# An output projection by seven quarter products, and the experts' rows turned back by TensorE

## The reference

```python
x = first_block(x, ...)
for i in range(2):                        # even layer, odd layer
    h_l = modulate(x, norm_mix[i], shift, scale)     # and the same for ctx
    m_l, m_c = even_mixer(...) @ w_out    # odd: only m_l is needed
    x = x + mod_l[2] * m_l                # the gated projection
    tok = modulate(x, norm_ffn[i], mod_l[3], mod_l[4])   # rms norm * (1 + scale) + shift
    f = hier_moe(tok, ...)                # router, then 16 experts, the best 2 of one group of 4
    x = x + mod_l[5] * f
```

## Time and profile before

| | |
|---|---|
| median of three runs | 2024.25 us (2022.09 to 2025.62) |
| profiled execution | 2020.34 us, its span 2018.6 us |
| mean granted clock of TensorE | 0.983 |
| even layer's projection, TensorE's matmuls | 1192.80 to 1279.80 us |
| odd layer's projection, its last matmul | ends at 1800.35 us |

### The profile page before, as it was taken

How to read it: one execution, slowest core, us unless ns; L and a number is a source line. 1 busy time by engine, 2 the same in 40 slices (tenths; PEclk the granted TensorE clock), 3 DMA queues, 4 the chain that set the end, 5 groups by cost and what they waited for, 6 DMA issues and landing times.

```text
span 2018.6 us, 28998 instructions
## 1 busy us (share of the span) xinstructions
PE 1891.2 (94%) x10950; PEld 1038.5 (51%) x10950; DVE 1187.0 (59%) x1908; ACT 642.7 (32%) x1274; POOL 262.8 (13%) x319
## 2 busy tenths in 40 slices
PE   7999999999999999999998999899997999989993
PEld 4554875544444444555645764633334678645330
DVE  2001777487787653358845644677757667456774
ACT  2011762200000001242313631256643556323551
POOL 3000110011111000012200012611102000051101
PEclk9999999999999999999999999999998989999997
DMA  8632100677666442311111011689965020148995
GB/s 260 169 84 84 54 12 22 219 253 258 235 236 239 147 174 97 133 42 42 42 42 63 1 36 73 266 335 362 363 239 202 1 84 2 35 157 354 387 416 199
DMA packets 108473, 323.89 MB, mean 160 GB/s; under 512 B 9063, under 2 KB 43015, under 8 KB 89904
## 3 DMA queue, kind: packets, MB, share of 16 engines
q1 hardware_dynamic: 77920, 190.56, 26.3%
q0 software_dynamic: 25024, 112.01, 15.6%
q10 hardware_dynamic: 5392, 19.47, 2.4%
HBM read 291.48 MB, written 35.76 MB: 162 GB/s over the span
## 4 chain that ended last, share of the span: by engine, by line
PE 71%; issue 7%; DMA 7%; DVE 6%; PEld 4%; PEldq 2%; ACT 1%; POOL 1%; POOLq 0%; DVEq 0%; SPq 0%; ACTq 0%
PE ps L3441 15%; PE ps L2060 6%; PE ps L466 6%; PE ps L2872 6%; PE ps L1190 5%; PE ps L1236 4%; PE ps L3242 4%; PE ps L1211 4%; DMA X<-moe_rows,row_token 4%; PE ps L364 3%; PE ps L335 2%; PE ps L2893 2%; PE ps L2036 2%; PEld ps L1783 2%; PE ps L1783 1%
## 5 line engine op out<-in xcount | busy, mean ns | idle before, releaser
L3441 PE MATMUL ps<-wide 128*128 128x512 f32 (+1 forms) x736 | 306.5, 575 | 1.9 <-issue 1.7
L3441 PEld LDWEIGHTS ps<-wide 128*128 128x128 f32 x736 | 138.3, 190 | 166.2 <-issue 164.1
L2872 PE MATMUL ps<-wide,X 128*32 x448 | 197.5, 594 | 2.1 <-DVE X L3043 2.1
L2872 PE MATMUL ps<-Z,X 128*32 128x512 f32 x1344 | 197.9, 594 | 0.0
L2060 PE MATMUL ps<-wide 128*128 128x512 f32 (+1 forms) x384 | 148.3, 543 | 0.5 <-issue 0.5
L1544 DVE SCALAR_TENSOR_TENSOR Z<-Z,wide 128x2048 f32<-128x2048 f32 x56 | 131.6, 2349 | 2.8
L1190 PE MATMUL ps<-T 64*128 64x256 f32 (+1 forms) x888 | 109.8, 377 | 8.7 <-DVE nm L1329 6.8
L1783 PE MATMUL ps<-wide 128*128 128x512 f32 x256 | 112.1, 595 | 2.1 <-issue 1.0
L744 ACT ACTIVATE T<-ps 128x512 f32<-128x512 f32 (+2 forms) x139 | 70.7, 536 | 128.2 <-PE ps L1783 109.8
L1261 ACT ACTIVATE T<-T,nm 128x768 f32<-128x768 f32 (+3 forms) x112 | 86.7, 775 | 77.5 <-DVE nm L1329 77.5
L2872 PEld LDWEIGHTS ps<-wide,X 128*32 128x32 f32 x448 | 47.0, 110 | 124.1 <-issue 124.1
(11 more groups left out here) (421 smaller groups left out, 3366.0 us busy)
## 6 DMA issues: line engine op xcount, KB each, us to landing
wide<-in_experts SPq DMA_DIRECT2D x64, 1024.0 KB, 9.7
Z<-in_mod_w POOLq DMA_DIRECT2D x32, 1024.0 KB, 5.2
T<-in_experts SPq DMA_DIRECT2D x32, 1024.0 KB, 11.8
X<-in_mod_w POOLq DMA_DIRECT2D x16, 1024.0 KB, 5.3
moe_out<-X ACTq DMA_DIRECT2D x28, 512.0 KB, 8.5
wide<-in_w_down SPq DMA_DIRECT2D x12, 1024.0 KB, 6.8
wide<-in_w_gate SPq DMA_DIRECT2D x22, 512.0 KB, 6.0
wide<-in_w_up SPq DMA_DIRECT2D x22, 512.0 KB, 6.9
```

The lines of the kernel that those rows point to most:

```text
L2872: last = pe.matmul(ps[rows, t % 2, :], mo.xT[:, c, rows], w_rows, start=(c == 0), stop=(c == DK - 1))
L3441: last = pe.matmul(self.gu.bank(u)[:, columns], w, self.rhs(c)[:, columns], start=(c == 0), stop=(c == DK - 1))
```

## The change

Three things are changed. **One**: in the even layer alone the gated projection becomes `GatedBySeven`. The product of the rows by `w_out` is split into quarters: even and odd row tiles by the two halves of the inner dimension, and `w_out` into four quarters of 512 x 512. Seven products of quarters, three of them of sums of quarters, are enough for the four quarters of the result. VectorE makes eight sums (S1 to S4 of the rows, 128x1536 each; T1 to T4 of the weights, 128x2048 each). ScalarE copies each P1 to the four places of the result that contain it; VectorE adds P2, P3, P6 and P5 from PSUM to these, multiplies each row by the gate and adds it to `X`, and then adds P7 and P4, each multiplied by the gate by itself. The adds form a chain: each waits for the one before. TensorE's order is P1 (before the meeting), P2, P3, P6, P5, then P7 and P4 pair by pair, with the turn of pair 0 after pair 1's, and that of pair 1 after pair 2's.

**Two**: in both layers GpSimd prepares no rows. TensorE turns the modulated `HT` back (`turn` of `RowStores`, units of four transposes, two units for a row tile): four units in `first_logits` in place of nine `keep_awake` matmuls, the others in the router in place of 16, and ahead of the drain that frees the slots. ScalarE copies each unit into the rows' place: four copies ahead of its takes of the last pair, two between the Exps, the rest after them. GpSimd stores the rows in the router's part, after `await_spilled`. The broadcast loads and VectorE's gains go. The wait for the gate rows moves from the stage's start to just ahead of the gating.

**Three**: the `late` transfer goes to ScalarE's queue, behind the last row's store.

The core of the diff:

```diff
 class GatedBySeven(Stage):                                 # new
+        self.PARTS = [(p, i) for p in ("P1", "P2", "P3", "P6", "P5") for i in range(n)] + [(p, i) for i in range(n) for p in ("P7", "P4")]
+    def tensor(self, pe):
...
+        self.after_sum(pe, "T4")
+        for i in range(n):
+            self.part(pe, "P7", i, self.s3, self.b12, 0 if i else 1)
+            self.part(pe, "P4", i, self.rows(1, 1), self.b21, 0 if i else 2)
+            if i:
+                self.norm.turn(pe, i - 1)
+        pe.drain().then_inc(k.weights_used, 2)
+        self.between(pe, self.norm)
+        self.norm.tensor(pe)
+    def vector(self, dve, ch):
...
+        for i in range(n):
+            gate = self.gates[:, 0 if 2 * i < ST else 1, :]
+            for row in (0, 1):
+                t = 2 * i + row
+                add(("gated", i, row), self.result(t), gate, ALU.mult)
+                add(("total", i, row), k.X[:, t, :], self.result(t))
+        for i in range(n):
+            gate, x = self.gates[:, 0 if 2 * i < ST else 1, :], k.X[:, 2 * i + 1, :]
+            self.after_part(dve, "P7", i)
+            multiply(("P7", i, "gated"), halves(self.product), twice("P7", i), halves(gate))
+            add(("P7", i, "total"), x, self.product)
+            if i:
+                self.norm.tile(dve, ch, 2 * i - 1)
+            self.after_part(dve, "P4", i)
+            multiply(("P4", i, "gated"), self.product[:, 0:512], self.bank("P4", i), gate[:, 0:512])
+            add(("P4", i, "total"), x[:, 0:512], self.product[:, 0:512])
+            self.norm.tile(dve, ch, 2 * i)
+            if i:
+                self.norm.take(dve, "dve", i - 1)
+        self.norm.tile(dve, ch, 2 * n - 1)
+        self.norm.vector(dve, ch)
 class RowAndTileNorm:
             if i == ST - 1:
                 act.dma_start(self.away[:, i, :], k.X[:, i, :]).then_inc(k.last_row_stored.sem, 16)
+                for dst, src in self.late:
+                    act.dma_start(dst, src).then_inc(k.last_row_stored.sem, 16)
...
-            if i == ST - 1:
-                for dst, src in self.late:
-                    pool.dma_start(dst, src).then_inc(k.small_landed.sem, 16)
 class RowStores(Stage):
+    def turn(self, pe, a, b):
+        k = self.k
+        for u in range(a, b):
+            t = self.norm.tiles[u // 2]
+            if u >= 2:
+                pe.wait_ge(k.rows_copied.sem, self.copied + u - 1)
+            for j in range(4):
+                last = pe.transpose(self.bank(u)[:, j * P:(j + 1) * P], k.HT[:, 4 * (u % 2) + j, t * P:(t + 1) * P], k.ident[:, :])
+            last.then_inc(k.rows_turned.sem, 1)
+    def copy(self, act, a, b):
...
+    def store(self, pool):
+        k = self.k
+        for i, t in enumerate(self.norm.tiles):
+            pool.wait_ge(k.rows_copied.sem, self.copied + 2 * i + 2)
+            pool.dma_start(self.rows_out[t * P:(t + 1) * P, :], self.place(i)).then_inc(k.rows_stored.sem, 16)
 class Router(Stage):
         for dst, src in self.rows_gate:
             pool.dma_start(dst, src).then_inc(k.small_landed.sem, 16)
+        self.stores.store(pool)
         self.stores.await_rows(pool)
...
         self.logits(pe, 0)
-        keep_awake(pe, k=self.k, bank=norm.banks.first + 3, n=9)
+        self.stores.last_banks_read(pe)
+        self.stores.turn(pe, 0, self.stores.FIRST)
...
         self.banks.filled(last)
+        self.stores.turn(pe, self.stores.FIRST, 2 * len(self.tiles))
         pe.drain().then_inc(k.places_free.sem, 1)
-        keep_awake(pe, k, 7, 16)
-        even.then = Linear(k, hT, DK, A["ev_w_out_2"][0], D, allt, gated_take(k.gatebc), ["dve"] * 12,
-                           norm=mod_sets(0, 1, True))
+        gate_rows = Loading(k, gate_loads(0, 2, 2))
+        even.then = GatedBySeven(k, A["ev_w_out_2"][0], allt, mod_sets(0, 1, True), k.gatebc, gate_rows.landed)
```

More of the change, by code:

```diff
@@ L321, in begin, with last_banks_read @@
                 pe.matmul(self.banks.bank(i)[:, 0:cn], self.lhs(k0 + c, t), w[:, c, :], start=(c == 0), stop=False)
+    def last_banks_read(self, pe):
+        self.banks.taken(pe, len(self.blocks) * len(self.tiles) - 2)
     def tensor(self, pe):
@@ L846, in scalar @@
                 self.take(act, "act", p)
+        if self.rows_copies:
+            self.rows_copies(act)
         for p in self.rest:
@@ L2394, in gpsimd, with landed, __init__ @@
             pool.dma_start(dst, src).then_inc(self.k.gate_rows.sem, 16)
[L2396 to L2397 removed]
+    def landed(self, eng):
+        eng.wait_ge(self.k.gate_rows.sem, self.base + 16 * len(self.pairs))
 class RowStores(Stage):
[L2405 removed]
+    FIRST = 4
+    def __init__(self, k, l, norm, rows_out, away):
         super().__init__(k)
         n = len(norm.tiles)
[L2408 to L2416 removed]
+        self.l, self.norm, self.rows_out, self.away = l, norm, rows_out, away
         self.consts = k.small_landed.reserve(64)
         self.stored, self.spilled = k.rows_stored.reserve(16 * n), k.spilled.reserve(16 * n)
+        self.turned, self.copied = k.rows_turned.reserve(2 * n), k.rows_copied.reserve(2 * n)
         self.n = n
@@ L2422, in place, with bank @@
         return self.k.Z[:, 5120 + D * i:5120 + D * (i + 1)]
+    def bank(self, u):
+        first = (1 if self.n == NT else 5) if u < self.FIRST else 5
+        return self.k.ps[:, first + u % 2, :]
+    def turn(self, pe, a, b):
[7 more added lines that the diff above has]
+            last.then_inc(k.rows_turned.sem, 1)
@@ L2424, in gpsimd, with await_copied @@
+    def copy(self, act, a, b):
+        k = self.k
+        for u in range(a, b):
+            act.wait_ge(k.rows_turned.sem, self.turned + u + 1)
+            act.activation(self.place(u // 2)[:, 512 * (u % 2):512 * (u % 2) + 512], self.bank(u), ACT.Copy).then_inc(k.rows_copied.sem, 1)
+    def await_copied(self, eng, u):
+        eng.wait_ge(self.k.rows_copied.sem, self.copied + u)
     def gpsimd(self, pool, ch):
         k, mo = self.k, self.k.mo
-        for dst, src in self.loads:
-            pool.dma_start(dst, src).then_inc(k.row_mods_landed.sem, 16)
@@ L2428, in gpsimd @@
         for dst, src in ((mo.iota, k.C["iota"]), (mo.token, k.C["token"]), (mo.before, k.C["before"]), (mo.pace, k.C["pace"][:, self.l, :])):
             pool.dma_start(dst, src).then_inc(k.small_landed.sem, 16)
-        pool.wait_ge(k.row_gains_ready.sem, self.ready + len(self.sets))
         for i, t in enumerate(self.norm.tiles):
-            gain, shift = self.sets[0 if t < ST else 1]
-            row = self.place(i)
             pool.wait_ge(k.norm_rows.sem, self.norm.rows + i + 1)
             pool.dma_start(self.away[:, t, :], k.X[:, t, :]).then_inc(k.spilled.sem, 16)
-            for c in range(0, D, 256):
-                ch.step(pool.tensor_tensor(row[:, c:c + 256], self.norm.hn[:, t, c:c + 256], gain[:, c:c + 256], ALU.mult))
-            ch.wait()
-            for c in range(0, D, 256):
-                ch.step(pool.tensor_tensor(row[:, c:c + 256], row[:, c:c + 256], shift[:, c:c + 256], ALU.add))
-            ch.wait()
-            pool.dma_start(self.rows_out[t * P:(t + 1) * P, :], row).then_inc(k.rows_stored.sem, 16)
@@ L2444, in vector @@
-    def vector(self, dve, ch):
+    def store(self, pool):
         k = self.k
-        dve.wait_ge(k.row_mods_landed.sem, self.landed + 16 * len(self.loads))
-        for gain, _ in self.sets:
-            dve.scalar_tensor_tensor(gain, gain, 1.0, self.gain, ALU.add, ALU.mult).then_inc(k.row_gains_ready.sem, 1)
+        for i, t in enumerate(self.norm.tiles):
+            pool.wait_ge(k.rows_copied.sem, self.copied + 2 * i + 2)
+            pool.dma_start(self.rows_out[t * P:(t + 1) * P, :], self.place(i)).then_inc(k.rows_stored.sem, 16)
@@ L2506, in tensor @@
         self.stores.norm.pair_taken(pe, len(self.tiles) // 2 - 1)
+        self.stores.await_copied(pe, self.stores.FIRST)
         self.logits(pe, 1)
@@ L2524, in scalar @@
             act.activation(to[:, 0:n, :], x[:, 0:n, :], ACT.Exp).then_inc(k.step_done.sem, 1)
+            if i == 0:
+                self.stores.copy(act, self.stores.FIRST, self.stores.FIRST + 2)
+        self.stores.copy(act, self.stores.FIRST + 2, 2 * n)
     def vector(self, dve, ch):
@@ L3840, in two_blocks, with row_stores @@
         k.expertgate = k.ring[:, 1:3, 1024:SLOT]
-        def row_stores(l, projection, sets):
-            mods = [[bc(scratch["mods"], D, (l * 2 + r) * 6144 + m * D) for m in (3, 4)] for r in range(sets)]
-            projection.row_stores = RowStores(k, l, projection.norm, bc(A["norm_ffn_2"], D, D * l), mods, scratch["h"][l], away)
-            return projection.row_stores
+        def row_stores(l, projection):
+            stores = RowStores(k, l, projection.norm, scratch["h"][l], away)
+            stores.last_banks_read = projection.last_banks_read
+            projection.norm.rows_copies = lambda act: stores.copy(act, 0, stores.FIRST)
+            projection.row_stores = stores
+            return stores
```

(2 more changed lines are left out.)

162 lines of the change are left out of this document (145 added, 17 removed).

## The result

The changed kernel takes 2030.64 us (median of 7 runs, 2028.27 to 2036.97); the kernel before, timed with it, 2022.09 us (7 runs). The ratio is 1.0037, 95% interval 1.0022 to 1.0051: slower by 4.4 to 10.3 us. The profiled execution has a span of 2033.9 us against 2018.6.

A forecast was written before the change was run, and what follows sets the result against it. It took TensorE to set the pace until 1280, then a relay between engines. Terms +3.1 +2.75 +0.4 +0.3 -1.0 -2.65 = +2.9 us, on the median of 2024.25, gave 2027; range 2018 to 2033.

The forecast's parts named there:

- The projection: Even layer to second logits: VectorE's twelve gating operations keep TensorE idle 11.7 us, eating the 10.3 saved; +3.1 us.
- The clock: Even layer after the idle stretch: half clock slows pair 2's products; +2.75 us, ends +1.6 and +5.1.
- the short wait: TensorE's 3.1 us wait ending at 842.6, kernel before: full clock back 3.3 us on, losing 1.65 at half speed.
- the long wait: TensorE's 9.2 us wait, kernel before: full clock back 6.9 us after resuming at 1528.5, losing 3.45 at half speed.
- rival (b): Even layer: clock stays low through pair 2, logits, part of dispatch; +9 to +12 us, 2030 to 2033; chance 0.17.
- Router: Even router and dispatch: small operations gain 1.2 us, turns and cold keep-awakes cost; between -1.1 and +1.7, taken +0.4.
- the odd layer: Odd layer: last turn and logits stay near their times, router gains 1.2 us, cold keep-awakes give back some; -1.0.
- The barrier: Ahead of the even layer: moved transfer frees the barrier, -1.85 us; with a clock that may not fall, -2.65.
- The stores: Router, both layers: six stores near 1297 to 1301, gather about 1314, leaving 10 us; nothing to +2, taken +0.3.
- rival (c): Router: rows land after the token list and the gather waits, +2 to +4 us, 2030; chance 0.05.

The follow-up runs named there:

- turns last: Changed kernel with the turns of pairs 0 and 1 behind the last P4: 1.0015; also with loads held for stores 1.0033, for gathers 1.0035.
- kept awake: Changed kernel with 48 matmuls on the identity in TensorE's idle stretch before the first turn: ratio 1.0036.
- stores late: Kernel before with the late transfer on ScalarE's queue and GpSimd's rows stored only behind the spilled tiles in the router: ratio 1.0029.
- loads held for the stores: Changed kernel with the third and fourth experts' gate and up weights issued only when the rows are stored: ratio 1.0065.
- stores first: Changed kernel with GpSimd issuing the rows' stores before it waits for the spilled tiles: ratio 1.0041.

## Why the prediction was right, and where it was mis-sized

The measured 2030.64 lies in the range (2018 to 2033) and 3.6 us over the forecast of 2027. The sign of the sum was right and its size was not: +2.9 was forecast, 8.5 lie between the medians, which is past the 0.2% that I had called no change. That the number lies in the range is in part luck: the kernel before came out 2.2 us under the median that I had added to, four terms came out some 3 us lower together than I had them, and one 7.8 higher. By the forecast's own terms:

**The projection: right in mechanism and size.** Forecast: TensorE idle 11.7 us before the turn of pair 0, twelve operations at 1.225, row 1 ready 77.4 us after the first product (1192.8 to 1270.2), second logits 3.1 later at full clock and 5.85 with the cold stretch. Measured: 11.19 us, 1.23, 77.1, and +4.9. The ten microseconds that TensorE saves are given back, because its next instruction in order waits for VectorE. The runs with the turns last get 0.7 to 2.6 of the 4.9 back and so show the order as a part of the cause; that the rest is VectorE's is read from its timeline.

**The clock: right, a little high.** I took +2.75; the run kept awake shows 1.9 at the first logits, from a return some 3.9 us after TensorE resumed, nearer the short wait's 3.3 than the long wait's 6.9. The 6.9 was misread. Between L928's eight transposes and its products TensorE stood idle for another 1.64 us of it:

```profile
1532.07 8.37 PE L3242 MATMUL ps<-wide 128*128 128x512 f32 x15 [1.64 <-issue]
```

The products ran cold from 1532.07 to near 1535.4, 3.3 us; the idle 1.64 us cost nothing more at either clock.

**The transposes and rival (b).** The clock did not stay low: it was back during pair 2's products, near 1276.3. Later, from 1296.70 to 1305.11 TensorE ran only turns of logits and rows, with holes, and the granted clock went from 0.50 (1298 to 1300) to 1.00 (1302 to 1304). The Trainium skill ("TensorE: Matmul & The Clock Gate", Part 4: PE-mode transpose) says that the full clock doesn't engage for transposes; here it did, so the measurement decides against that rule for these float32 turns.

**Router: the gain as counted, its cause not shown.** Forecast +0.4 and, in the odd layer, part of -1.0; measured -0.5 and -1.0 from logits to list. The four small operations took 0.82 us, as I had counted (0.84), and the turns cost less than I had allowed. But the gain needs no turned rows: the run with the stores late has it too (19.6 and 18.7), with GpSimd still making the rows. Without stores to issue in between, GpSimd's last product ends 3.6 us after the second logits there, before 6.5. Nor does it always stay: in seven of the ten runs with the rows turned back the odd piece is 19.2 to 19.8. In the one with the loads held for the stores, 28 `keep_awake` matmuls took 8.92 us in place of 8.10, and VectorE, done as early, waited 2.90 us in place of 1.65 for the matmul behind them.

**The barrier: right.** Forecast -1.85 and half of 1.6 for the clock. Measured -1.92 at the barrier and 1.4 more within the next 8 us, where the clock was 1.00 at once.

**The stores: the step that failed.** "Six stores of 512 KB come near 1297 to 1301 ... That leaves 10 us; nothing to +2, I take +0.3 for both layers." The place was near (1299 to 1306), the landing was not. The gathers wait 3.7 us longer in the even layer and 4.6 in the odd, and the piece from there to the first expert is 1.0 longer and 1.2 shorter: +8.1 in place of +0.3. I had given this (rival (c)) 0.05 and one layer's price. The error was to ask when the stores are issued, and not what the transfer engines do at that time. They were 28% busy in the last 30 us of the projection and had 8 MB of expert weights to bring from its end on. Of the six even stores of the kernel before, GpSimd issued four ahead of these loads; rows that are turned back after the projection can't be stored so soon. 3 MB and 2 MB at the 396 GB/s of the even stretch are 7.9 and 5.3 us of transfer time. No term of the forecast has the second price of the wait: the first experts run cold, 1.6 us in the even and 2.7 in the odd layer. The stretches from there to the next projection and to the last matmul are 0.9 and 1.8 us longer than before; other runs differ by as much there, so I add nothing for it.

With the terms put right, +4.9 for the projection and its clock, -0.5 for the router, -1.3 for the odd layer, -3.3 for the barrier and +8.1 for the stores, the sum is +7.9, beside 8.5 between the medians and 7.5 by the ratio. That the terms add up so is not shown by the totals: with and without the seven products they are the same, 1.0037.

## What to carry to other kernels

When work moves from one engine to another, follow its transfers too: a store that leaves a stretch with idle transfer engines for one in which they are full can cost most of its transfer time (here 5.1 and 4.6 us, of 7.9 and 5.3), and holding other loads back handed the queue to the next reader in all five runs that tried it. Before counting saved matmuls, write out the in-order queue of the engine that gets the adds, and look at which instruction of TensorE waits for its end; put what doesn't need those results ahead of it.

## What I had not expected of the hardware

GpSimd beside VectorE cost far more than the average add had shown (1.06 against 0.69). With GpSimd's products running, an add of 128x1024 took 3.80 us in place of 1.23, and a normed row (one tensor and a scalar for each partition) 3.31 in place of 0.75; GpSimd's four products of 256 columns beside that row took 2.76 together.

Keeping TensorE busy through the idle stretch did not buy the cold time back: the granted clock fell some 14 us later, over the logits at 1287, behind a wait of 2.41 us that had cost nothing of the kind in the changed kernel. One profile each doesn't tell whether the one brought on the other: the same wait cost 1.7 us in the run with the stores first, and nothing in the run with the loads held for the stores (1.93 us for the logits).
